# Attention on one core: values out of the 384-column query-key product, put in unit order over DRAM, with a new order in a step and written-out supersteps

## What is computed

```
qkv = (x @ w_in).reshape(b, s, 3, N_GROUPS, ATTN_HEADS, ATTN_HEAD_DIM)      # 3 groups, 16 heads, 64 each
for g, (window, dilation) in enumerate(((128, 1), (512, 4), (2048, 16))):
    q = rms_norm(qkv[:, :, 0, g], q_gain[g]) * (ATTN_HEAD_DIM ** -0.5)
    k = rms_norm(qkv[:, :, 1, g], k_gain[g])
    o, l = dilated_window_attention(q, k, qkv[:, :, 2, g], rel_bias[:, g], window, dilation)
wts = softmax(stack(lses), axis=0)
y = einsum('gbsh,gbshe->bshe', wts, stack(outs)) ; return y @ w_out
```

## Time and profile before

| | us |
|---|---|
| median of 3 runs | 3331.82 |
| lowest and highest | 3330.32, 3334.62 |
| the profiled execution | 3333.34 |
| its span | 3331.6 |
| mean granted TensorE clock, as a share of 2.4 GHz | 0.977 |
| busy in the span: PE matmuls | 3162.4 (95%) |
| weight loads (PEld) | 2672.2 (80%) |
| DVE | 1337.3 (40%) |
| ACT | 1107.3 (33%) |
| POOL | 824.0 (25%) |

### The profile page before, as it was taken

How to read it: one execution, slowest core, us unless ns; L and a number is a source line. 1 busy time by engine, 2 the same in 40 slices (tenths; PEclk the granted TensorE clock), 3 DMA queues, 4 the chain that set the end, 5 groups by cost and what they waited for, 6 DMA issues and landing times. The chain is left out here.

```text
span 3331.6 us, 48256 instructions
## 1 busy us (share of the span) xinstructions
PE 3162.4 (95%) x17466; PEld 2672.2 (80%) x17466; DVE 1337.3 (40%) x3725; ACT 1107.3 (33%) x3002; POOL 824.0 (25%) x598
## 2 busy tenths in 40 slices
PE   4999999999999995999999999899877999999999
PEld 3888888888888883878888888778665788888887
DVE  6446554555556554341313133531064431313131
ACT  4555555555555553321111112211254211111020
POOL 3333333333233310222222222222211222222221
PEclk9999999999999996999999999999898999999999
DMA  2112121221212114111111111111201111111112
GB/s 97 39 38 62 41 59 40 62 54 47 56 45 62 41 28 153 50 45 50 51 47 48 51 45 51 36 47 45 82 32 51 45 51 45 51 51 45 51 51 76
DMA packets 89904, 177.01 MB, mean 53 GB/s; under 512 B 25515, under 2 KB 55870, under 8 KB 89662
## 3 DMA queue, kind: packets, MB, share of 16 engines
q1 hardware_dynamic: 87358, 169.63, 16.4%
q10 hardware_dynamic: 2304, 4.20, 0.3%
HBM read 160.67 MB, written 13.12 MB: 52 GB/s over the span
## 5 line engine op out<-in xcount | busy, mean ns | idle before, releaser
L69 PE MATMUL ps_qk<-w_hi,attn_hT_hi 128*128 128x256 f32 x1536 | 439.1, 286 | 23.9 <-DVE attn_hT_lo L213 9.7
L915 POOL TENSOR_TENSOR first_w_lo<-first_raw,first_w_hi 128x1024 fp32r<-128x1024 f32 x96 | 231.5, 2411 | 886.0 <-ACT first_w_hi L911 886.0
L71 PE MATMUL ps_qk<-w_hi,attn_hT_lo 128*128 128x256 f32 x1536 | 437.6, 285 | 0.0
L70 PE MATMUL ps_qk<-w_lo,attn_hT_hi 128*128 128x256 f32 x1536 | 437.4, 285 | 0.0
L857 POOL TENSOR_TENSOR w_lo<-raw,w_hi 128x384 fp32r<-128x384 f32 x192 | 193.6, 1009 | 660.3 <-ACT w_hi L602 660.3
L915 POOL TENSOR_TENSOR second_w_lo<-second_raw,second_w_hi 128x1024 fp32r<-128x1024 f32 x72 | 172.3, 2393 | 620.6 <-ACT second_w_hi L911 620.6
L69 PEld LDWEIGHTS ps_qk<-w_hi,attn_hT_hi 128*128 128x128 f32 x1536 | 295.9, 193 | 28.2 <-issue 13.9
L70 PEld LDWEIGHTS ps_qk<-w_lo,attn_hT_hi 128*128 128x128 f32 x1536 | 296.6, 193 | 0.4
L71 PEld LDWEIGHTS ps_qk<-w_hi,attn_hT_lo 128*128 128x128 f32 x1536 | 296.4, 193 | 0.0
L69 PE MATMUL first_ps<-first_hid_hi,first_w_hi 128*128 128x512 f32 x640 | 250.9, 392 | 33.5 <-DVE first_hid_lo L1241 33.5
L635 ACT ACTIVATE prob<-ps_s,neg_max 128x128 f32<-128x128 f32 (+1 forms) x384 | 156.3, 412 | 362.4 <-DVE neg_max L726 362.4
(11 more groups left out here) (276 smaller groups left out, 6844.6 us busy)
## 6 DMA issues: line engine op xcount, KB each, us to landing
raw<-in_wqkv SPq DMA_DIRECT2D x192, 192.0 KB, 2.3
first_raw<-in_w SPq DMA_DIRECT2D x64, 512.0 KB, 3.4
second_raw<-in_w SPq DMA_DIRECT2D x64, 512.0 KB, 3.4
w_bc<-share_dram SPq DMA_DIRECT2D x48, 256.0 KB, 4.2
first_raw<-in_vo_pieces SPq DMA_DIRECT2D x16, 512.0 KB, 3.4
bias<-bias_dram SPq DMA_DIRECT2D x16, 256.0 KB, 3.4
yT_dram<-o_g SPq DMA_DIRECT2D x8, 512.0 KB, 3.1
first_raw<-in_attn_wo SPq DMA_DIRECT2D x8, 512.0 KB, 3.5
```

What stands on the lines that cost most here:

```text
L69: pe.matmul(out, a_hi, b_hi, start=first, stop=False)
L70: pe.matmul(out, a_hi, b_lo, start=False, stop=False)
L71: return pe.matmul(out, a_lo, b_hi, start=False, stop=last)
L915: pool.tensor_tensor(self.lo[:, n % 2, :], self.raw[:, n % self.RAW, :], self.hi[:, n % 2, :].bitcast(F32), ALU.subtract).then_inc(self.lo ...
```

## The change

- The product of a token tile has all 384 columns of query, key and value (`ps_qk[..., 0:W3]`), so it is 24 products of 384 columns. `ps_v`, its six products a step, `vT`, its copies and the value transpose go.
- ACT copies the value columns of `ps_qk` to one of two slots `v_out` (in `ring`). SP stores each tile to `v_dram`, and after four tiles waits for both slots' stores and loads the half back into `v_raw`, in unit order: one transfer for groups 0 and 1, two for group 2, in pieces of 512 bytes.
- ACT casts `v_hi` from `v_raw`, ahead of `w_hi`; `v_lo` is made by POOL, between `w_lo` and `rs`, and no longer by DVE.
- PE does half of the products, turns the tile before, weighs the values (now of the unit before the last), does the other half, turns the last unit's probabilities, and computes scores.
- ACT's turned tiles (`qk_hi`) come straight after the exponentials, ahead of outputs and `w_hi`; DVE's (`qk_lo`) straight after the maxima, ahead of the merge.
- All 27 supersteps are written out; the loop is gone.

The core of the diff; the bodies of the moved parts are as before:

```diff
-    for st in range(LOOP_FIRST):
-        for j in range(TT):
-            step(0, st, j)
-    with eng.Fori(0, LOOP_COUNT) as i:
...
+    for st in range(LAST_SUPER + 1):
         for j in range(TT):
+            step(st, j)
...
+        def v_loads(sec):
+            return 64 * (sec // NG) + (16, 32, 64)[sec % NG]
+        def unit_order(sec, half):
+            rows = v_dram[sec % 2, half * HALF:(half + 1) * HALF]
+            if sec % NG == 0:
+                return [(v_raw[:, sec % 2, 4 * half:4 * half + 4, :], rows.rearrange("(u p) c -> p u c", p=P))]
+            if sec % NG == 1:
+                dest = v_raw[:, sec % 2].rearrange("p (r n) c -> p r n c", n=2)[:, :, half, :]
+                return [(dest, rows.rearrange("(i r) c -> i r c", r=4))]
+            src = rows.rearrange("(i u b) c -> b i u c", b=2, u=TT)
+            return [(v_raw[64 * b + 32 * half:64 * b + 32 * half + 32, sec % 2], src[b]) for b in range(2)]
+        def halves_needed(sec, u):
+            if sec % NG == 0:
+                return {0: [0], 4: [1]}.get(u, [])
+            if sec % NG == 1:
+                return {0: [0], 1: [1]}.get(u, [])
+            return [0, 1] if u == 0 else []
...
# SP, first in a step
+                if 1 <= T <= TT * SECTIONS:
+                    sec, t = divmod(T - 1, TT)
+                    if sec >= 2 and t == 0:
+                        for half in range(2):
+                            sp.wait_ge(v_in[half], v_loads(sec - 2))
+                    sp.wait_ge(v_kept, T)
+                    sp.dma_start(v_dram[sec % 2, t * P:(t + 1) * P, :], v_out[:, t % 2, :]).then_inc(v_stored[t % 2], 16)
+                    if t % 4 == 3:
...
+                        if sec >= 2:
+                            sp.wait_ge(v_lo_done, TT * (sec - 1))
+                        for slot in range(2):
+                            sp.wait_ge(v_stored[slot], 16 * (T // 2))
+                        for dest, src in unit_order(sec, t // 4):
+                            sp.dma_start(dest, src).then_inc(v_in[t // 4], 16)
...
# PE
-                        mm = split_matmul(pe, ps_qk[j % 2][:, 0:2 * P],
+                        mm = split_matmul(pe, ps_qk[j % 2][:, 0:W3],
                                           hT_hi[:, k, j * P:(j + 1) * P], hT_lo[:, k, j * P:(j + 1) * P],
-                                          w_hi[:, par, k, 0:2 * P], w_lo[:, par, k, 0:2 * P], k == 0, k == KT - 1)
+                                          w_hi[:, par, k, :], w_lo[:, par, k, :], k == 0, k == KT - 1)
...
+                if st == 0:
+                    products(range(KT))
+                    turn_tiles()
+                else:
+                    products(range(KT // 2))
+                    turn_tiles()
+                    weigh_values()
+                    products(range(KT // 2, KT))
+                    turn_probabilities()
+                    scores()
...
# ACT
+                        act.copy(v_hi[:, (U - 1) % 3, :], v_raw[:, sec % 2, u, :]).then_inc(v_hi_done, 1)
...
+                        act.activation(sq[:], ps_qk[j % 2][:, 0:2 * P], ACT.Square).then_inc(squared, 1)
+                        if T >= 2:
+                            act.wait_ge(v_stored[j % 2], 16 * (T // 2))
+                        act.copy(v_out[:, j % 2, :], ps_qk[j % 2][:, 2 * P:W3]).then_inc(v_kept, 1)
...
+                if st == 0:
+                    weights()
+                    squares_and_values()
                     turned_tiles()
...
+                exponentials()
+                turned_tiles()
+                outputs()
+                unit_values()
...
+                weights()
+                squares_and_values()
+                turned_probabilities()
...
# DVE
+                maxima()
+                turned_tiles()
+                merge_step(st, j)
+                variances()
+                turned_probabilities()
+                normalise()
...
# POOL, between w_lo and rs
+                if has_unit(st, j, 1):
+                    sec, u = unit(st, j, 1)
+                    slot = (U - 1) % 3
+                    pool.wait_ge(v_hi_done, U)
+                    pool.tensor_tensor(v_lo[:, slot, :], v_raw[:, sec % 2, u, :], v_hi[:, slot, :].bitcast(F32),
+                                       ALU.subtract).then_inc(v_lo_done, 1)
```

More of the change, by code:

```diff
@@ L332, in __init__ @@
         self.prob = sb("prob", [P, 2, 2, 2 * P])
-        self.x_tiles = [b[:, i, :] for b in (self.vT, self.o_g0, self.w_bc) for i in range(2)]
+        self.x_tiles = [b[:, i, :] for b in (self.v_raw, self.o_g0, self.w_bc) for i in range(2)]
         self.x_tiles += [self.o_g2[:, 0, :], self.prob[:].rearrange("p a h k -> p (a h k)")]
@@ L503, in step, with products @@
                 par = st % 2
-                if st < SECTIONS:
-                    if st >= 1 or j >= 2:
+                def products(ks):
+                    if st >= SECTIONS:
+                        return
+                    if T >= 2 and ks[0] == 0:
                         pe.wait_ge(qkn_done, T - 1)
-                    for k in range(KT):
+                        pe.wait_ge(v_kept, T - 1)
+                    for k in ks:
                         if st == 0 and j % 4 == 0:
@@ L526, in step @@
                             mm = pe.transpose(ps_t[:, a * P:(a + 1) * P], qkn[:, (j - 1) % 2, a * P:(a + 1) * P], ident[:])
[L527 to L531, removed]
+                    if rows:
                         pe.wait_ge(exp_done, U - 1)
@@ L535, in step, with weigh_values @@
                     mm.then_inc(turned, 1)
[L536 to L540, removed]
+                def weigh_values():
                     if has_unit(st, j, 2):
+                        sec, u = unit(st, j, 2)
+                        g = sec % NG
+                        whole = TT * sec + u
                         pe.wait_ge(p_hi_done, U - 1)
                         pe.wait_ge(p_lo_done, U - 1)
[L544 to L561, removed]
@@ L569, in step, with turn_probabilities @@
+                        for b in range(first, 2):
+                            slot = (whole - 1 + b) % 3
+                            mm = split_matmul(pe, ps_o[:, 0:2 * P], v_hi[:, slot, :], v_lo[:, slot, :],
+                                              pT_hi[:, b, :], pT_lo[:, b, :], b == first, b == 1)
+                        mm.then_inc(pv_done, 1)
+                def turn_probabilities():
                     if has_unit(st, j, 1):
+                        sec, u = unit(st, j, 1)
+                        g = sec % NG
@@ L570, in step @@
                         pe.wait_ge(exp_done, U)
[L571 to L594, removed]
+                        if has_unit(st, j, 2):
+                            pe.wait_ge(p_hi_done, U - 1)
+                            pe.wait_ge(p_lo_done, U - 1)
@@ L617, in step @@
                 par = st % 2
[L618 to L625, removed]
@@ new lines, in turned_tiles @@
+                def turned_tiles():
+                    if 1 <= T <= TT * SECTIONS:
+                        act.wait_ge(turned, T)
+                        sec, t = divmod(T - 1, TT)
+                        g = sec % NG
+                        for a in range(2):
+                            ins = act.activation(perm_dest(qk_hi[:, sec % 2, a, :], g, t * P, P),
+                                                 perm_view(ps_t[:, a * P:(a + 1) * P], g, P), ACT.Copy,
+                                                 scale=gains[:, a, g:g + 1])
+                        ins.then_inc(turn_hi, 1)
@@ new lines, in turned_tiles @@
+                def turned_tiles():
+                    if j == 1 and 2 <= st <= SECTIONS and (st - 2) % NG < 2:
+                        if T <= TT * SECTIONS:
+                            dve.wait_ge(turn_hi, T)
+                        else:
+                            dve.wait_ge(turned, T)
+                        if st >= 3:
+                            dve.wait_ge(rows_out, 16 * (2 * ((st - 2) // NG) + (st - 2) % NG))
+                        dve.tensor_copy(stat_rows[:], ps_t[0:4 * TT, 3 * P:4 * P]).then_inc(rows_done, 1)
+                    if 1 <= T <= TT * SECTIONS:
+                        dve.wait_ge(turn_hi, T)
+                        sec, t = divmod(T - 1, TT)
+                        g = sec % NG
+                        for a in range(2):
+                            ins = dve.scalar_tensor_tensor(
+                                perm_dest(qk_lo[:, sec % 2, a, :], g, t * P, P),
+                                perm_view(ps_t[:, a * P:(a + 1) * P], g, P), gains[:, a, g:g + 1],
+                                perm_dest(qk_hi[:, sec % 2, a, :].bitcast(F32), g, t * P, P), ALU.mult, ALU.subtract)
+                        ins.then_inc(turn_lo, 1)
```

334 lines of the change are left out of this document (166 added, 168 removed).

## The result

The changed kernel takes **3392.26 us** (median of 4 runs, 3388.14 to 3393.16), the kernel before 3331.68 in the runs beside it: ratio 1.0178, with a 95% interval of 1.0161 to 1.0196. It is 60.6 us slower; 84 were forecast, with 3416, and the range was 3350 to 3475.

A forecast was written before the change was run, and what follows sets the result against it. PE bounds the old kernel's attention; the new order makes a loop through ACT, POOL and DVE the bound. Loop +80, merge +14, loop turns -10 give +84 us: 3416 us, range 3350 to 3475.

The forecast's parts named there:

- The circle: Loop through ACT, POOL and DVE in attention: 6.86 us a two-block step, 6.39 a one-block step, above PE's 6.27; +80 us.
- The merge: In 35 merge steps, DVE's large instructions slow POOL's w_lo by 0.39 us each: +14 us, bounds 0 and 25.
- My upper bound: Merge term's high bound: 25 us, 0.7 for each of 35 steps, if POOL waits until DVE's instruction is over.
- The sum: Whole kernel: 80 + 14 - 10 = +84 us, 3416 us as a median, 2.5% slower.
- Written-out supersteps: Attention's loop: its two turns go, 2 x 5.0 us, so -10 us.
- The transfers at nothing: Values' store and load over DRAM: 8.4 us for both legs, hidden by a distance of two steps; cost nothing.
- PE's part: PE's two-block attention step: 24 products of 384 columns at 0.18 us; new sum 6.27 us, 0.21 less than 6.48.
- PE's rest: PE in attention steps: idle some 0.6 us before the qkn transposes, or 10%.
- rival 1: Attention: PE stays the bound at 6.27 us a step, so the kernel gets faster, 3283 us; chance 0.12.
- The clock: PE's clock in attention should hold at 1.00 despite PE's rests.

The follow-up runs named there:

- e1: The changed kernel with POOL making the power before v_lo (order w_lo, rs, v_lo); 3345.26 us, ratio to before 1.0042.
- e4: The changed kernel with w_hi last on ACT and POOL's order rs, v_lo, w_lo from the second superstep on; 3315.7 us, ratio 0.995.
- e10: e3 with one more POOL instruction, 128x128, between w_lo and the power; 3323.18 us, beside 3322.72 of e3.
- e2: The changed kernel with DVE's merge back ahead of its turned tiles; 3362.68 us, ratio 1.0094.
- e8: e5 with the values' transfers over DRAM doubled; 3297.63 us, against 3296.62 of e5.
- e3: The kernel before with all 27 supersteps written out and nothing else changed; 3322.72 us, ratio 0.9974.
- e6: e5 with PE's 24 products of a tile in one piece instead of two halves; 3313.14 us, ratio 0.9945.
- e9: e5 with SP's load of a weight tile issued one step later; 3288.72 us, ratio 0.9872.
- e5: The changed kernel with the changes of e4 and e2 together; 3296.62 us, ratio 0.9895.

## Why the prediction was right, point by point

**The circle** was right as a mechanism. e1 takes one of its terms away, and the time came to within 1 us of what the sum said. e4 takes three away and came to within 11, by two larger errors against each other. e10 shows that a term alone, in a circle with slack, costs nothing. Its size was too large. I had 6.86 and 6.39 us; plain steps are 6.64 and 6.16. Two terms hold the difference: w_lo kept POOL for 0.96 us where I took 1.08, and v_lo for 0.43 where I took 0.54, both from the mean over the group of four w_lo in the earlier trace rows. A mean over a group hides what is in it. Asked for its members, the timelines of POOL and DVE in the kernel before show (the second line is two of the four):

```profile
44.95 1.00 POOL L857 TENSOR_TENSOR w_lo<-raw,w_hi 128x384 fp32r<-128x384 f32 x1
45.90 1.96 POOL L857 TENSOR_TENSOR w_lo<-raw,w_hi 128x384 fp32r<-128x384 f32 x2
...
47.82 1.45 POOL L857 TENSOR_TENSOR w_lo<-raw,w_hi 128x384 fp32r<-128x384 f32 x1
...
46.89 1.52 DVE L234 SCALAR_TENSOR_TENSOR bias<-vT,attn_norm_gain,total 128x512 f32<-128x512 f32 x1
```

Three stand 0.95 to 0.96 apart. The fourth took 1.45 and ended 0.86 behind the end of a DVE instruction with two inputs in SBUF (48.41): it is the lock of the merge steps, in the trace of before, inside the very row from which I took 1.08. All other terms (0.59, 1.04, 1.46, and 2.16 for exponentials, qk_hi, outputs and v_hi) came within 0.01. In group 1 one-block steps take 6.30 us and not 6.16. This term gave 39 us for 80. I had also counted superstep 23 as full, whose circle has no w_hi and w_lo: another 5 us too many. Superstep 13 took 54.07 us, near the 54.4 that I forecast, but by luck: 52.07 is the circle, and the rest the merge.

**The merge** was mis-sized the other way: 36 us for 14. The step that failed is "I take this 0.39 for 35 steps", from POOL's 1.66 us beside DVE's work. What the earlier trace rows leaves out is how much of DVE's instruction was left:

```profile
34.68 0.74 DVE L234 SCALAR_TENSOR_TENSOR bias<-o_g,attn_norm_gain,total 128x512 f32<-128x512 f32 x1
```

It ended at 35.42, 0.53 us after POOL's start, and POOL's subtraction ended 1.13 behind it, where it takes 1.27 alone. The delay is what is left of DVE's instruction, less 0.14. So 0.39 did show a full lock, with little left of it. In the merge steps the same sum gives 1.53 - 0.14 = 1.39 for the w_lo that took 2.41 in place of 1.01. This is the rule of the Trainium skill ("SBUF — State Buffer", "Who interferes with whom") that the prediction cited and set aside.

My upper bound, 25 at 0.7 us for each of 35, met the 24.5 of the large instructions, but by luck: those of 1.22 us cost 0.41, and those that read a group in permuted order last 1.99 (L900) and cost 1.05 to 1.21. The merge's small instructions, 5.5 us, were not in my sum. In e2, with the merge elsewhere, 30 of the 36 us went.

**The sum.** The two errors partly cancelled: -41 for the circle and +22 for the merge, and -5 for superstep 23, leave the 60 us of the measurement. The total looks better than its parts.

**Written-out supersteps**: -10 forecast, -8 measured alone (e3). Its interval, -12 to -5 us, holds the 10 us that its trace shows at the turns.

**The transfers at nothing**: right (e8). A store takes 2.2 us and a load 3.1, not the 4.2 that I allowed for each.

**PE's part**: 384-column products start 0.177 us apart (763.12 to 765.24 for twelve), where I took 0.18. But the whole step of PE is 6.35 us, where I summed 6.27, although the products are 0.08 us less than I took. So some 0.16 us lie elsewhere. Changes between kinds of matmul are a part of it: e6, with one fewer, gained 0.04. The rest I didn't place. PE's rest in a plain step is 6.64 less 6.35, 0.29 us and not the 0.6 forecast. Between the earlier trace rows and e9, which differ on PE as the forecast had it, the two-block step gains 0.13 us; e9 stands 34 us below e3. So rival 1, with 3283, describes a kernel that exists, e9 at 3289; the changed kernel isn't it because its ACT and POOL order hands PE's gain, and more, to the circle.

**The clock** stayed at 1.00, as taken, with PE at 94%.

## What to carry to other kernels

When an instruction is moved on an engine that isn't the bound, list the circle that it closes: through every engine in written order, back to itself one step on. Add up the starts; the step can't be shorter, however idle each engine looks. Work that feeds only later steps (w_hi, w_lo, v_lo here) goes last in an engine's step, and what the next step waits for (the power) first. With the merge and SP's wait moved too, this turned a change that lost 1.8% into one that gains 1.3%. And look at what a wait on SP holds back: in e5 a prefetch waited for work that had moved to the end of a step, and took unrelated transfers with it.

## What I had not expected

A DVE instruction with both inputs in SBUF keeps POOL's off entirely: w_lo took 2.41 us beside one of 1.99 and 1.43 beside one of 1.22, ending 0.88 and 0.87 behind it. The kernel before had the same in its norm stage (1.45, ending 0.86 behind). In the changed kernel two more merge steps agree: the w_lo beside L893 and L907 end 0.87 and 0.88 behind. And on POOL two ready instructions stand closer than their durations: 0.96 apart for one that lasts 1.01, and 0.43 for 0.47.
